# Two second-type layers of a diffusion-style network on one core: no barriers inside the mixing part, projections begun in the tail of the stage before

## What is computed

```python
h = rms(x, g_mix[l]) * (1.0 + sc1) + sh1
parts = jnp.split(h @ w_in[l], IN_SPLITS, axis=-1)
...
y_a = gqa_attention(qa, ka, va) @ w_branch_a[l]
...
y_b = dilated_attention(qs, kss, vs) @ w_branch_b[l]
gate_a = jax.nn.sigmoid(parts[3 + 3 * N_B])
gate_b = jax.nn.sigmoid(parts[4 + 3 * N_B])
mixed = gate_a * y_a + gate_b * y_b
x = x + gt1 * (mixed @ w_out[l])
h2 = rms(x, g_mlp[l]) * (1.0 + sc2) + sh2
x = x + gt2 * (jnp.square(jax.nn.relu(h2 @ w_ff1[l])) @ w_ff2[l])
```

## Time and profile before

| | us |
|---|---|
| median of 3 runs | 4056.66 |
| lowest and highest | 4052.11, 4063.92 |
| the profiled execution, whole | 4064.24 |
| its span, first to last instruction | 4062.2 |
| PE busy with matmuls | 3663.4 |
| mean granted clock of PE, share of full | 0.934 |

### The profile page before, as it was taken

One profiled execution on the slowest core, in us unless ns is written; L12 is line 12 of the kernel. 1 busy time (PEld: TensorE's weight loads), 2 busy tenths in 40 slices (PEclk: granted clock), 3 DMA queues, 4 the chain that ended last, 5 costly groups with the idle time before them and its releaser, 6 DMA issues.

```text
span 4062.2 us, 46458 instructions
## 1 busy us (share of the span) xinstructions
PE 3663.4 (90%) x17778; PEld 2864.5 (71%) x17778; DVE 2115.5 (52%) x2923; ACT 1183.0 (29%) x1474; POOL 239.0 (6%) x268
## 2 busy tenths in 40 slices
PE   8998888999999997789997888988999889889998
PEld 3766656788887765567885566776887557677787
DVE  6445334766656455356666455246666445344333
ACT  2234233211213243332223233223223233223222
POOL 0000000100100000000000000000000000000100
PEclk9988888999999988989998899999999899799999
DMA  7210100322221111114441011124443111122222
GB/s 312 80 42 32 49 28 21 119 110 103 98 109 69 63 42 52 45 68 153 163 163 71 21 54 53 63 93 157 164 156 114 38 44 63 43 93 83 94 96 99
DMA packets 51297, 357.35 MB, mean 88 GB/s; under 512 B 5840, under 2 KB 7504, under 8 KB 9552
## 3 DMA queue, kind: packets, MB, share of 16 engines
q1 hardware_dynamic: 36320, 261.11, 17.5%
q10 hardware_dynamic: 14832, 94.22, 6.3%
HBM read 353.21 MB, written 2.10 MB: 87 GB/s over the span
## 4 chain that ended last, share of the span: by engine, by line
PE 57%; issue 25%; DVE 12%; ACT 4%; DMA 1%; POOL 0%; ACTq 0%; DVEq 0%; POOLq 0%
PE pair L519 29%; PE pair L890 5%; PE pair L540 4%; PE pair L795 2%; DVE arena L1811 2%; PE pair L552 2%; PE pair L956 2%; PE pair L531 1%; PE pair L653 1%; DVE w_lo L1751 1%; PE pair L813 1%; PE pair L840 1%; PE pair L1020 1%; PE pair L912 1%; PE pair L1066 1%
## 5 line engine op out<-in xcount | busy, mean ns | idle before, releaser
L519 PE MATMUL pair<-h_hi,w_hi 128*128 128x512 f32 (+5 forms) x2048 | 704.7, 379 | 44.9 <-POOLq L2326 34.1
L519 PE MATMUL pair<-h_lo,w_hi 128*128 128x512 f32 (+5 forms) x2048 | 696.9, 375 | 0.0
L519 PE MATMUL pair<-h_hi,w_lo 128*128 128x512 f32 (+5 forms) x2048 | 694.6, 374 | 0.0
L1751 DVE TENSOR_TENSOR w_lo<-raw,w_hi 128x2048 fp32r<-128x2048 f32 x225 | 515.9, 2293 | 340.4 <-ACT w_hi L1216 337.9
L1216 ACT ACTIVATE w_hi<-raw 128x2048 fp32r<-128x2048 f32 x225 | 429.1, 1907 | 722.9 <-PE pair L519 646.8
L1767 DVE SCALAR_TENSOR_TENSOR x<-pair,mod,x 128x512 f32<-128x512 f32 (+1 forms) x408 | 271.7, 690 | 448.0 <-PE pair L519 429.3
L519 PEld LDWEIGHTS pair<-h_hi,w_hi 128*128 128x128 f32 (+2 forms) x2048 | 358.5, 188 | 125.4 <-issue 52.7
L519 PE MATMUL pair<-u_hi,w_hi 128*128 128x512 f32 (+3 forms) x1200 | 405.4, 375 | 37.0 <-DVE x L1767 19.8
L519 PEld LDWEIGHTS pair<-h_hi,w_lo 128*128 128x128 f32 (+2 forms) x2048 | 357.1, 188 | 74.7 <-issue 0.2
L519 PEld LDWEIGHTS pair<-h_lo,w_hi 128*128 128x128 f32 (+2 forms) x2048 | 358.4, 188 | 72.8 <-issue 0.3
L519 PE MATMUL pair<-u_hi,w_lo 128*128 128x512 f32 (+3 forms) x1200 | 400.7, 371 | 0.0
(11 more groups left out here) (284 smaller groups left out, 4864.5 us busy)
## 6 DMA issues: line engine op xcount, KB each, us to landing
raw<-in_wt_dram SPq DMA_DIRECT2D x226, 1024.0 KB, 4.8
arena<-in_modw_dram ACTq DMA_DIRECT2D x78, 1024.0 KB, 4.8
arena<-in_modw_dram SPq DMA_DIRECT2D x18, 1024.0 KB, 7.0
arena<-in_fconst_dram ACTq DMA_DIRECT2D x2, 2688.0 KB, 9.3
x<-in_xt_dram SPq DMA_DIRECT2D x1, 3072.0 KB, 16.4
arena<-in_brope_dram ACTq DMA_DIRECT2D x4, 640.0 KB, 3.9
out_dram<-x SPq DMA_DIRECT2D x1, 2048.0 KB, 7.2
arena<-in_headw_dram ACTq DMA_DIRECT2D x8, 208.0 KB, 2.4
```

The source lines that it names most:

```text
L519: mm = pe.matmul(pp[p][0:m, lo:hi], a[0:rows, k * width + c0:k * width + c0 + m], b[0:rows, k, lo:hi], start=(k == 0 and i == 0), stop=(k ...
L1751: dve.tensor_tensor(w_lo[slot][:], raw[slot][:], w_hi[slot][:].bitcast(F32), ALU.subtract)\
```

## The change

The four barriers inside the mixing part of each second-type layer go; 8 in all. In their place:

- In gqa, `maxima` takes a part of its four units. The 16 units are laid out as 2, product and rope products, 4, value product and rope products, 4, value product, 6. Before, it was 4, product and rope, 4, value and rope, value, 8.
- The last step of the gqa outputs has the first dilated product ahead of it and the second behind it. The DMA of the rope tables is issued before the 16 steps, that of the masks in round 0 of `dilated`; `high(3)` moves behind the first scaling of `dilated`.
- In round 1 of `dilated`, the first tile of `gates` is used between the maxima. ACT and DVE convert the second tile of `gates` there too.
- The gate products turn through four PSUM banks instead of two pairs. PE waits for all four to be read and for `low(1)` before the branches.
- The output projection begins with `first_jobs`, which waits for each remainder `h_lo` by itself.

```diff
-                def maxima(j):
-
-                    pe.wait_ge(rope_done, t.next(rope_done) + 2)
+                def maxima(j, part=range(NT)):
+
+                    if 0 in part:
+                        pe.wait_ge(rope_done, t.next(rope_done) + 2)
                     halves = gqa_halves(j)
-                    for i in range(NT):
+                    for i in part:
 
...
-                maxima(0)
+                early, late = range(2), range(2, NT)
+                maxima(0, early)
                 w = tile()
                 bank_product(w, 0, 256, 0, job_act)
                 bank_rope(1, g_sq[1], g_qg[1])
-                maxima(1)
+                maxima(0, late)
+                maxima(1, early)
                 values(w, 0, 1, job_act)
                 bank_rope(0, g_sq[0], g_qg[0])
+                maxima(1, late)
+                maxima(2, early)
                 values(w, 1, 0, tile_used)
-                maxima(2)
+                maxima(2, late)
                 maxima(3)
 
...
-                for s in range(4 * NT + 1):
-                    if s < 4 * NT:
-                        scores(s)
+                for s in range(4 * NT):
+                    scores(s)
                     if s:
                         outputs(s - 1)
 
-                pe.wait_ge(st_free, t.now(st_free, 2))
+                w = tile()
+                bank_product(w, 0, 256, 0, job_act)
+                outputs(4 * NT - 1)
+                bank_product(w, P, 256, 1, tile_used)
 
             def dilated():
-                barrier()
-                pe.wait_ge(const_in["dilated"], t.next("dilated", 32))
...
                 for pr in range(2):
-                    w = tile()
-                    bank_product(w, 0, 256, 0, job_act)
                     if pr:
+                        w = tile()
+                        bank_product(w, 0, 256, 0, job_act)
                         outputs(0, 3)
                     for i in range(6):
-                        if i + 1 < 6:
+                        if pr + i and i + 1 < 6:
                             if i % 2:
                                 w = tile()
                             bank_product(w, (i + 1) % 2 * P, 256, (i + 1) % 2, job_act if i % 2 else tile_used)
                     if pr == 0:
                         w = tile()
                         values(w, 0)
+
+                        pe.wait_ge(st_free, t.now(st_free, 2))
                         maxima(0, 0)
                         maxima(1, 1)
                         values(w, 1)
...
+                        w = tile()
                         maxima(0, 1)
                         maxima(1, 0)
+                        bank_product(w, 0, 256, 0, job_act)
                         maxima(2, 1)
                         maxima(3, 0)
+                        bank_product(w, P, 256, 1, tile_used)
                         turn(1)
                         by_key(0, 0)
                         by_key(1, 1)
...
-                for _ in range(8):
+                for i in range(1, 8):
                     w = tile()
                     for c in range(2):
-                        feature_job(w, KC, P, c * P, P, 256, H, S, c, tile_used if c else job_act)
-                barrier()
+                        bank_product(w, c * P, 256, (2 * i + c) % 4, tile_used if c else job_act)
+
+                for p in range(4):
+                    pair_read(p)
+
+                pe.wait_ge(dve_pe, t.next(dve_pe))
...
-                barrier()
-                for _ in range(4):
+                take_pair(2)
+                take_pair(3)
+                first_jobs(tile(), (pp[2], pp[3]), S, (job_dve, tile_used))
+                for i in range(1, 4):
                     w = tile()
                     for c in range(2):
-                        feature_job(w, KC, P, c * P, P, 256, H, S, c, tile_used if c else job_dve)
+                        feature_job(w, KC, P, c * P, P, 256, H, S, (2 * i + c + 2) % 4, tile_used if c else job_dve)
...
+                act.dma_start(arena[:, 0:B0], io["brope"][1]).then_inc(const_in["dilated"], 16)
...
                 sums(3)
-                high(3)
                 t.next("st_base", 4 * NT)
 
             def dilated():
-                barrier()
-                act.dma_start(arena[:, 0:B0], io["brope"][1]).then_inc(const_in["dilated"], 16)
-                act.dma_start(d_mask, io["mask"]).then_inc(const_in["dilated"], 16)
...
                 for pr in range(2):
                     project(0)
+                    if pr == 0:
+
+                        act.wait_ge(dve_act, t.next(dve_act))
+                        act.activation(u6_hi[:, 3, :], g_y[1], ACT.Copy).then_inc(act_dve, 1)
                     for i in range(6):
                         if i + 1 < 6:
                             project(i + 1)
+                        if pr == 0 and i == 1:
+                            act.dma_start(d_mask, io["mask"]).then_inc(const_in["mask"], 16)
                         rope_root(r_r[i % 2])
...
                     else:
+                        split()
                         shifts()
...
             def gates():
-                barrier()
                 for i in range(8):
-                    split()
+                    if i:
+                        split()
                     for c in range(2):
                         job(last=c == 1)
-                        act.activation(gate[i // 4][:, 2 * (i % 4) + c, :], pp[c][:, 0:S], ACT.Sigmoid)\
-                           .then_inc(pair_free[c], 1)
+                        b = (2 * i + c) % 4
+                        finish(act.activation(gate[i // 4][:, 2 * (i % 4) + c, :], bank(b), ACT.Sigmoid), pair_free[b],
+                               *([gates_in] if i == 7 and c else []))
                 exp_table()
-                barrier()
                 for i in range(4):
                     split()
                     for c in range(2):
 
                         act.wait_ge(dve_act, t.next(dve_act))
                         act.activation(h_hi[:, 2 * i + c, 0:S], mx_f[2 * c], ACT.Copy).then_inc(act_dve, 1)
-                barrier()
...
-                maxima(0)
+                early, late = range(2), range(2, NT)
+                maxima(0, early)
                 rope(3)
-                maxima(1)
+                maxima(0, late)
+                maxima(1, early)
                 rope(4)
+                maxima(1, late)
                 maxima(2)
                 maxima(3)
...
                         split()
+
+                        dve.wait_ge(const_in["mask"], t.next("mask", 16))
                         maxima(0, 0)
...
                         turned(1)
+                        split()
                         by_key(0, 0)
...
             def gates():
-                barrier()
-                for i in range(8):
+                for i in range(7):
                     split()
-                barrier()
+
+                dve.wait_ge(gates_in, t.next(gates_in))
+                t.next(h_ready, KC)
...
-                        dve.tensor_tensor(h_lo[:, j, 0:S], a, H32[:, j, 0:S], ALU.subtract)
-                barrier()
+                        dve.tensor_tensor(h_lo[:, j, 0:S], a, H32[:, j, 0:S], ALU.subtract).then_inc(h_ready, 1)
                 for i in range(4):
                     split()
                     for c in range(2):
                         job(last=c == 1)
-                        residual(2 * i + c, S, c, 0, squares=True)
...
-                pool.wait_ge(const_in["dilated"], t.next("dilated", 32))
+                rope_cos(range(5), g_qg, g_qc)
+                pool.wait_ge(const_in["dilated"], t.next("dilated", 16))
+                rope_cos(range(2), r_qg, r_qc)
+
+                pool.wait_ge(st_free, t.next(st_free, 4) + 2)
                 pool.memset(d_v[:, :, :, 64:128], 1.0)
-                rope_cos(12, r_qg, r_qc)
-
-                barrier()
-                barrier()
-                barrier()
+                rope_cos(range(2, 12), r_qg, r_qc)
```

22 lines of the change are left out of this document (11 added, 11 removed).

## The result

| | before | changed |
|---|---|---|
| median of the runs | 4057.05 | 3991.09 |
| lowest and highest | 4052.11, 4063.92 | 3983.15, 4001.00 |
| the profiled execution, whole | 4064.24 | 3983.15 |
| ratio of the runs, with its 95% interval | | 0.9836 (0.9811 to 0.9862) |

The account below looks back on a forecast made before the run. PE, busy 90% of the span, was taken as the bound, so only its idle time or clock loss pays. 1.8 - 12 - 18.2 - 10.7 = -39.1 us per layer, -78 for two, from 4056.7 to 3978; range 3946 to 4004.

Parts of the forecast that it names:

- Part 1: Maxima in gqa: spreading them puts both value products behind waits, at the lower clock; +1.8 us per layer.
- rival 1: Value products of gqa: the clock stays up through both, 13.1 us less per layer, 3952 us; chance 0.25.
- Part 2: From gqa into `dilated`: 13.13 us idle and a cold start go, a 2.6 us wait comes; -12 us per layer.
- its late next: Second tile of `dilated`: its `w_lo` stands on DVE behind the last gqa remainder, so PE waits 2.6 us.
- Part 3: Second round of `dilated` and the gate products: 140.5 us becomes 122.3, -18.2 us per layer, bounds 13 and 22.
- The new wait: Third gate tile: its conversion takes 13.8 us while PE has two products, 10.9, so PE waits 2.9 us.
- the cold start behind it: Gate products behind the wait at the third gate tile: 1.5 us for a cold start that may come.
- the chain around `turn`: Second round of `dilated`: `turn` 1.4 us, then the chain through DVE and ACT to the shift rows, 3.6.
- The rest of the round: Second round of `dilated`, from the shift rows to the last output: 20.0 us before, partly at the lower clock, taken as 18.5.
- Two maxima 1.6, product 5.4: Second round of `dilated`, behind its first wait: two maxima, then a gate product replacing the wait of 4.22 us.
- Part 4: Branches and output projection: 1.3 + 7.8 + 2.2 - 0.6 us saved by shorter waits and no cold start; -10.7 per layer.
- Rival 3: Third gate tile: its wait keeps 14 gate products at 1.2 GHz, 36.5 us slower per layer, 4130 us; chance 0.02.

Follow-up runs that it names:

- run with the product in two pieces: The changed kernel with the first gate tile's second product cut into 12 and 12 matmuls, the second piece behind `turn`: 3972.7 us, ratio 0.9804.
- the run with the barriers back: The changed kernel with two barriers inside gates put back, ahead of the branches and ahead of `first_jobs`: 4006.6 us, ratio 0.9886.
- the run with the gqa order alone: The kernel before, all barriers kept, gqa maxima on PE as 2, product and rope, 2, value, 2, rope, 2, value, 8: 4019.4 us, ratio 0.9918.
- three edits of a few lines: The changed kernel plus value products' cover in gqa, second gate product in two pieces, and two conversions issued earlier: 3920.5 us, ratio 0.9677.

## Why the prediction was right, and where it was off

The table sets each part against the traces, in us per layer. To be rid of the spread of single executions it takes the mean over all profiled runs in which the part in question was as before, or as changed (in brackets how many stretches each).

| part | stretch | before | changed | measured | forecast |
|---|---|---|---|---|---|
| 1 | gqa maxima | 55.60 (4) | 55.09 (10) | -0.5 | +1.8 |
| 2 | from the transposed maxima to the head of round 1's maxima | 214.1 (4) | 202.9 (12) | -11.3 | -12 |
| 3 | from there to the branches | 141.7 (4) | 128.9 (8) | -12.9 | -18.2 |
| 4 | branches, and the output projection | 45.8 (4) + 45.9 (4) | 38.2 (14) + 43.8 (14) | -9.7 | -10.7 |

The sum is -34.4 per layer, -69 for both. The medians have -66, with -56 to -77 in the interval, so the table and the medians agree, and the saving of 78 that was forecast lies just outside it.

**Part 1** was right in kind: no gain, since each value product stood behind a wait. The two in the trace of before already told it. Of the ten stretches with the new order, six took 57.1 to 57.3 us, where 57.0 was worked out; in the other four (51.2 to 52.4) one of the two products was back at the upper clock within its first 1.2 us. What I had not weighed is that this falls one way or the other from one stretch to the next, in one kernel and one execution too. What the mean shows of rival 1, which had a chance of 0.25, is 4 products of 20. That part 1 came out 2.3 us better than forecast is luck of this kind; the mechanism that was forecast is the one of the six.

The Trainium skill, page "TensorE: Matmul & The Clock Gate", section "HAM oscillation — how this bites in real kernels", was drawn on for this part; it says that short bursts between waits start throttled. All 24 value products behind a wait of 2.7 to 3.8 us began at the lower clock, and 20 of them ran their whole length there (16 of the 20 in the new order, all 4 in the old). The first unit of maxima behind such a wait, though, often still ran at 1.00: in layer 2 of the changed kernel the clock fell 1.1 us after PE had gone on. Of the 16 value products with no such wait ahead 14 ran at 1.00 throughout, and 2, which came behind other products at the lower clock, ran only their first half microsecond there.

**Part 2** was right, and so was its late next: the wait at the second tile was 2.64 us in all of these runs, forecast 2.6, worked out from the end of PE's gqa and ACT's distance to it. The stretch from there to the head of round 1 became 0.9 us longer on the mean (133.5 against 132.5); it is about what lay between the 12.9 of the working and the 12 taken. The clock fell at that wait in 9 of the 12 stretches. No run puts this barrier back alone, so part 2 is read from stretches only.

**Part 3** is where the sum failed. 122.3 us were worked out, and 128.9 is the mean of eight stretches. The new wait (3.12 against 2.9), the cold start behind it (1.8 against 1.5) and the chain around `turn` (4.6 against 1.4 + 3.6) came as worked out. The mis-sized terms are these:

- "The rest of the round took 20.0 ... I take 18.5, between 16 and 20." It took 22.3 on the mean (23.84 and 22.29 in the profile shown), +3.9. The 18.5 assumed that the products ahead keep the clock up. They don't in any of the eight (granted clock 0.64 to 0.77), since the wait of 2.69 us at the shift rows stands between. And the trace of before had the answer: this stretch took 20.0 us in layer 2, at granted clock 0.78, and 23.9 in layer 3, at 0.64. I had read one layer of the two:

```profile
2539.46:2559.47 20.01, 19.55 (x132) 14.92 (x132) 5.36 (x5) 4.51 (x5) 0.00 (x0) 0.78 0.00 1
3469.83:3493.75 23.92, 23.46 (x132) 17.57 (x132) 5.36 (x5) 4.51 (x5) 0.00 (x0) 0.64 0.00 1
```

- "Two maxima 1.6, product 5.4": behind the wait of 2.91 they took 2.8 and 7.2 us in layer 2 (6.0 in layer 3), in part made good by the next two maxima, 2.8 instead of 3.5. With the wait and the second product it is 20.4 on the mean instead of 18.8, +1.6. A cold start stands here too, and I had priced one only at the third gate tile.
- The 14 gate products with their wait took 81.5 instead of 80.0, +1.5; 0.6 of it are the products themselves, 76.2 at the upper clock where 75.6 were taken.

Less 0.4 in the chain that is +6.6 us; the stretch before is 1.2 longer on the mean than the 140.5 that I took from layer 2, and 5.3 us per layer are missing. The run with the product in two pieces shows that the first term is clock and not dependence: same work, 16.28 us.

**Part 4** was right: 7.6 us in the branches and the wait behind them (1.3 + 7.8 - 0.6, 8.5, were worked out) and 2.2 of clock in the projection (2.2), by stretches and by the run with the barriers back. The four projections before took 46.62 and 45.31 us here and 46.7 and 45.2 in the run with the gqa order alone, so one layer's cold start is not the mean. **Rival 3** (gate products at 1.2 GHz) did not come: behind the wait of 3.12 they lost 1.8 us and were back at the upper clock.

For both layers, part 3 saved 11 us less than forecast, parts 2 and 4 together some 3 less, and part 1 came out 5 better: that makes 9 of the 13 us between 3978 and 3991. Without the luck of part 1 the median would lie near 3996. What remains is within the spread: executions of one kernel here differ by up to 28 us (3990.7 to 4018.2 with the barriers back), and the profile after, 8 us below its own median, flatters the change where the profile before lay 7.6 above.

What is not settled is what lets the clock fall and rise. Why the same value product behind the same wait is soon back at the upper clock in one case out of six no run tells. Nor is a long wait needed for a fall. In layer 2 before, the largest of several short waits among the last maxima was 1.32 us, and the real scores behind it lost 3.4 us; the same fall stands in 8 of the 20 layers traced. In layer 2 of the changed kernel the clock fell in round 0 of `dilated` with no wait at all, behind narrow matmuls (7 of 20), and the 24 matmuls there took 7.15 us instead of 5.57. The rows are the last maxima and the scores before, then the narrow matmuls, the product behind them and the next such product of the changed kernel:

```profile
2293.06:2302.31 9.25, 6.32 (x41) 3.25 (x40) 8.65 (x8) 0.00 (x0) 0.00 (x0) 1.00 0.00 0
2302.31:2309.97 7.66, 7.66 (x21) 3.19 (x20) 0.00 (x0) 3.22 (x4) 0.00 (x0) 0.55 0.00 0
```

```profile
2421.00:2425.14 4.14, 4.14 (x45) 3.13 (x45) 1.10 (x1) 1.57 (x3) 0.00 (x0) 1.00 0.00 0
2425.14:2432.29 7.15, 7.15 (x26) 5.83 (x25) 3.30 (x2) 2.40 (x2) 0.00 (x0) 0.76 0.15 38
2436.44:2442.01 5.57, 5.57 (x26) 4.61 (x25) 1.23 (x1) 0.00 (x0) 0.00 (x0) 1.00 0.01 3
```

## What to carry to other kernels

When a barrier goes, work out from rows what is late next and what clock the work behind that wait will run at; both of the new waits here were right to 0.2 us, and most of the error came from work behind an old wait that had stayed. Read each stretch in every layer before you take its length, above all where its granted clock lies between the two levels. And look for waits like those of 2.7 to 3.4 us here right ahead of narrow matmuls: half a wide product put there was worth 6.1 us of clock on the mean (16.3 us instead of 20.2 to 23.8), and three edits of a few lines brought another 64 us by the ratios, as much as the whole change.
